# One core, four layers: a six-place weight ring that runs across the layers, boundary transposes inside the last products, every lo split on VectorE

## The reference

```python
for l in range(2):                                   # block A
    z = rms_norm(x, norm_mix[l]) @ w_in[l]           # 1024 -> 4768 columns
    c_q, c_kv, k_pe, hq, hf, hi, hg, g_a, g_b = split(z)
    y_a = mla_mixer(c_q, c_kv, k_pe, ...) @ w_proj_a[l]      # 8 heads of 96, causal
    y_b = hgrn2_mixer(hq, hf, hi, hg, ...) @ w_proj_b[l]     # 4 heads of 128, decay per channel
    x = x + (sigmoid(g_a) * y_a + sigmoid(g_b) * y_b) @ w_out[l]
    h = rms_norm(x, norm_ffn[l])
    x = x + (silu(h @ w_gate[l]) * (h @ w_up[l])) @ w_down[l]   # 1024 -> 2816 -> 1024
for l in range(2):                                   # block B
    q, k, v, z, xbc, dt = split(rmsnorm(x, ...) @ w_in_2[l])    # 1024 -> 3344 columns
    attn = dilated_attention(rotary(q), rotary(k), v)
    y = ssd_chunked(silu(conv4(xbc)), softplus(dt), ...) * silu(z)
    x = x + concat(attn, rmsnorm(y)) @ w_out_2[l]
    x = x + swiglu(rmsnorm(x, ...), w_gate_2[l], w_up_2[l], w_down_2[l])
return rmsnorm(x, final_norm)
```

## Time and profile before

| what | value |
|---|---|
| median of 3 runs | 1556.57 us (1555.61 to 1557.41) |
| profiled execution, span | 1555.7 us |
| PE busy / PEld busy | 1479.3 us (95%) / 1258.1 us (81%) |
| DVE / ACT / POOL busy | 946.3 us (61%) / 787.6 us (51%) / 198.3 us (13%) |
| mean granted TensorE clock | 0.988 |
| moved from HBM | 243.52 MB, 157 GB/s over the span |

### The profile page before, as it was taken

How to read it: one execution, slowest core, us unless ns; L and a number is a source line. 1 busy time by engine, 2 the same in 40 slices (tenths; PEclk the granted TensorE clock), 3 DMA queues, 4 the chain that set the end, 5 groups by cost and what they waited for, 6 DMA issues and landing times.

```text
span 1555.7 us, 23669 instructions
## 1 busy us (share of the span) xinstructions
PE 1479.3 (95%) x7525; PEld 1258.1 (81%) x7525; DVE 946.3 (61%) x1306; ACT 787.6 (51%) x1228; POOL 198.3 (13%) x146
## 2 busy tenths in 40 slices
PE   4998999999989799999999999999999999999997
PEld 4877887888888688788888988888887988888886
DVE  3577775555455887655554497755554487755554
ACT  4574445444366554544445665544444565554443
POOL 1033300000010432000002232000002223000000
PEclk9998999999999999999999999999999999999999
DMA  6653255655555523465655343465655343455553
GB/s 183 197 155 109 82 163 162 192 191 185 171 174 153 159 84 122 150 202 185 191 183 173 103 133 119 136 191 188 189 189 161 112 139 110 149 172 184 185 189 107
DMA packets 180347, 245.92 MB, mean 158 GB/s; under 512 B 21008, under 2 KB 131984, under 8 KB 180240
## 3 DMA queue, kind: packets, MB, share of 16 engines
q1 hardware_dynamic: 180240, 244.61, 50.3%
HBM read 243.52 MB, written 1.05 MB: 157 GB/s over the span
## 4 chain that ended last, share of the span: by engine, by line
PE 82%; DVE 8%; issue 5%; ACT 3%; SPq 1%; DMA 0%; DVEq 0%; ACTq 0%; POOL 0%; POOLq 0%
PE acc L578 15%; PE acc L580 15%; PE acc L579 15%; PE misc L578 9%; PE misc L580 9%; PE misc L579 9%; PE misc L643 2%; DVE w_lo L1289 2%; PE misc L736 2%; DVE arena L1612 2%; PE misc L859 1%; PE misc L653 1%; DVE arena L1370 1%; PE misc L807 1%; ACT w_hi L928 1%
## 5 line engine op out<-in xcount | busy, mean ns | idle before, releaser
L1289 DVE TENSOR_TENSOR w_lo<-w_raw,w_hi 128x1024 fp32r<-128x1024 f32 (+3 forms) x420 | 504.7, 1210 | 333.3 <-ACT w_hi L928 331.0
L928 ACT ACTIVATE w_hi<-w_raw 128x1024 fp32r<-128x1024 f32 (+3 forms) x472 | 481.2, 1029 | 321.0 <-PE misc L580 162.8
L578 PE MATMUL acc<-w_hi,h_hi 128*128 128x512 f32 (+3 forms) x832 | 315.7, 379 | 38.4 <-DVE w_lo L1289 23.9
L580 PE MATMUL acc<-w_hi,h_lo 128*128 128x512 f32 (+3 forms) x832 | 307.6, 370 | 0.0
L579 PE MATMUL acc<-w_lo,h_hi 128*128 128x512 f32 (+3 forms) x832 | 307.3, 369 | 0.0
L578 PE MATMUL misc<-w_hi,h_hi 128*128 128x512 f32 x640 | 253.8, 396 | 0.5
L580 PE MATMUL misc<-w_hi,h_lo 128*128 128x512 f32 x640 | 249.7, 390 | 0.0
L579 PE MATMUL misc<-w_lo,h_hi 128*128 128x512 f32 x640 | 249.2, 389 | 0.0
L578 PEld LDWEIGHTS acc<-w_hi,h_hi 128*128 128x128 f32 x832 | 160.4, 193 | 66.3 <-DVE w_lo L1289 27.5
L1832 POOL TENSOR_TENSOR w_lo<-w_raw,w_hi 128x1024 fp32r<-128x1024 f32 (+2 forms) x52 | 113.3, 2186 | 766.7 <-ACT w_hi L928 766.7
L578 PE MATMUL acc<-w_hi,st_hi 128*128 128x512 f32 (+1 forms) x456 | 177.9, 390 | 0.9 <-DVE w_lo L1289 0.9
(11 more groups left out here) (199 smaller groups left out, 1360.9 us busy)
## 6 DMA issues: line engine op xcount, KB each, us to landing
w_raw<-in_w_in SPq DMA_DIRECT2D x92, 512.0 KB, 4.4
w_raw<-in_w_gate SPq DMA_DIRECT2D x176, 256.0 KB, 2.9
w_raw<-in_w_up SPq DMA_DIRECT2D x176, 256.0 KB, 3.1
w_raw<-in_w_down SPq DMA_DIRECT2D x88, 512.0 KB, 3.3
w_raw<-in_w_out SPq DMA_DIRECT2D x40, 512.0 KB, 3.4
w_raw<-in_w_in SPq DMA_DIRECT2D x32, 388.0 KB, 3.2
w_raw<-in_w_in SPq DMA_DIRECT2D x16, 336.0 KB, 5.0
w_raw<-in_w_proj_a SPq DMA_DIRECT2D x8, 512.0 KB, 3.4
```

The lines of the kernel that those rows point to most:

```text
L578: pe.matmul(dst, hi[:, k, cols], rhs_hi, start=first, stop=False)
L580: return pe.matmul(dst, lo[:, k, cols], rhs_hi, start=False, stop=last)
L928: act.activation(w_hi[:, s % RING, 0:w], w_raw[:, s % RING, 0:w], ACT.Copy)\
L1289: dve.tensor_tensor(w_lo[:, s % RING, 0:w], w_raw[:, s % RING, 0:w], w_hi[:, s % RING, 0:w].bitcast(F32), ALU.subtract)\
```

## The change

The layer loops and the feed-forward loop are written out, so that all four layers are one straight program and slots have one running number g. The ring gets six places and `LOOK` becomes 5; splits for the next layer's slots are made during the last feed-forward steps. GpSimd makes no lo any more. SP loads the next layer's parameters in feed-forward step 4. nT0 and nT1 of the next layer stand ahead of the last three matmuls of the last down product, nT2 and nT3 inside or behind the first slot of the layer; mT2 and mT3 stand behind the first gate/up slot. The last down product does its left half for both slots first. `lbc` is computed once. The scratch for dynamic transfers is set to 2048.

```diff
-RING = 4
+RING = 6
-POOL_LO = ({0, 1, 2, *range(ORD[0].slot_no["gate1", 1], ORD[0].slot_no["gate3", 3] + 1, 2)},
-           {0, 1, 2, *range(ORD[1].slot_no["xd0", 0], ORD[1].slot_no["wo1", 1] + 1, 2)})
-LOOK = 3
+LOOK = RING - 1
+        for i in (2, 3):
+            self.before["misc", f"mT{i}"] = self.ffn0 + 1
...
-        nT0 nT1 nT2 nT3 qkv0 qkv0 qkv1 ...
+        nT0 nT1 qkv0 nT2 nT3 qkv0 qkv1 ...
...
@@ SP: ahead of each load; feed-forward loads
+            def freed(g):
+                if g >= RING:
+                    sp.wait_ge(*DV_.of("lo", g - RING))
...
+                    if i == 4 and layer != LAYERS[-1]:
+                        params(LAYERS[LAYERS.index(layer) + 1])
@@ PE: run_slot, gate_up, last_down
+                    if name == "qkv0" and k == 2:
+                        shared(layer, "nT2")
+                        shared(layer, "nT3")
...
+                        if i == 0 and q == 1:
+                            shared(layer, "mT2")
+                            shared(layer, "mT3")
...
+            def last_down(g):
+                pe.wait_ge(*DV_.at(layer, "fT10"))
+                pe.wait_ge(*DV_.of("lo", g))
+                half_down(g, 10, 0)
+                pe.wait_ge(*DV_.of("lo", g + 1))
+                half_down(g + 1, 10, 0).then_inc(*PE.mark("x_half"))
+                half_down(g, 10, 1).then_inc(*PE.slot("used", g))
+                half_down(g + 1, 10, 1, (0,)).then_inc(*PE.mark("x_tile"))
+                if layer != LAYERS[-1]:
+                    ...
+                    shared(after, "nT0")
+                    shared(after, "nT1")
+                half_down(g + 1, 10, 1, (1,)).then_inc(*PE.slot("used", g + 1))
@@ ACT: norm_operand
-                if name == "mT0":
-                    split_until(layer, ORD[layer[0]].chunk_end("wo1") + LOOK)
-                b = wait_bank(layer, name)
-                if kind == "mT":
-                    act.wait_ge(*name_at(PE, layer, "used", ORD[layer[0]].chunk_end("wo1") - 1))
+                if kind == "nT" and i < 2:
+                    split_until(layer, 3)
+                    act.wait_ge(*PE.at(layer, name))
+                    b = misc[ORD[layer[0]].turn[name] % 4]
+                else:
+                    b = wait_bank(layer, name)
@@ DVE: split_until, end of feed_forward, top of body_a
+                n = min(BASE[layer] + n, TOTAL)
+                for g in range(split[0], n):
+                    dve.wait_ge(*AC.of("hi", g))
...
+                dve.wait_ge(*PE.at(layer, "x_half"))
+                residual(layer, [(0, t, acc[t]) for t in range(NT)], ["x_ffn0", "x_ffn1"])
+                if layer != LAYERS[-1]:
+                    ...
+                    norm_operand(after, "nT0")
+                dve.wait_ge(*PE.at(layer, "x_tile"))
+                residual(layer, [(1, 0, acc[2])], ["x_ffn2"])
+                dve.wait_ge(*PE.of("used", BASE[layer] + o.slots - 1))
+                residual(layer, [(1, 1, acc[3])], ["x_ffn3"])
...
-                dve.tensor_copy(lbc[:, 0, :], lbs[:, bass.ds(l, 1), :].rearrange("p a h -> p (a h)"))\
-                    .then_inc(*DV_.mark())
@@ POOL: body_a, the last of its calls
-                    split_until(layer, o.before["misc", f"oH{t}"] + LOOK)
```

More of the change, by code:

```diff
@@ L76, in mark, with slot, of, at @@
         if name is not None:
-            self.table[self.block, name] = self.k
+            self.table[self.layer, name] = self.k
         return self.sem, 1
[L80 to L123, removed]
+    def slot(self, what, g):
+        self.k += 1
+        self.table[what, g] = self.k
+        return self.sem, 1
+    def of(self, what, g):
+        return self.sem, (self.old[what, g] if self.old else 1)
+    def at(self, layer, name):
+        return self.sem, (self.old[layer, name] if self.old else 1)
+    def now(self, layer):
+        return self.sem, self.k
 class Chunk:
@@ L859, in turn, with half_down @@
                             tr = pe.transpose(misc[0][:, at:at + P], f_act[:, t, kk * P:(kk + 1) * P], ident)
-                    tr.then_inc(*PE.mark(f"fT{step}"))
-                def down(s, step, first=False, last=False, j=None, between=None):
-                    pe.wait_ge(*DV_.at(layer, f"fT{step}", j))
+                    tr.then_inc(*PE.mark(f"fT{i}"))
+                def half_down(g, i, half, tiles=range(NT)):
+                    for t in tiles:
+                        at = half * 512
+                        mm = product(acc[2 * half + t][:, :], stat["st"], (g - base) % 2 + (2 if i == 10 else 0), t,
+                                     w_hi[:, g % RING, at:at + 512], w_lo[:, g % RING, at:at + 512],
+                                     i == 0 and (g - base) % 2 == 0, i == 10 and (g - base) % 2 == 1)
+                    return mm
@@ L896, in feed_forward @@
[L896 to L913 removed]
+                down(g + 8, 0)
@@ new lines, in feed_forward @@
+                turn(1)
+                g += 10
+                for i in range(2, FSTEPS - 1):
+                    gate_up(g, i, behind=f"f{i - 1}")
+                    down(g + 4, i - 1)
+                    turn(i)
+                    g += 6
+                gate_up(g, FSTEPS - 1, behind=f"f{FSTEPS - 2}")
+                down(g + 4, FSTEPS - 2, between=FSTEPS - 1)
+                last_down(g + 6)
+            pe.wait_ge(shifted, 1)
+            for layer in LAYERS:
+                PE.begin(layer)
+                for item in ORD[layer[0]].plan:
+                    if item[0] == "slot":
+                        run_slot(layer, item[1], item[2])
+                    elif item[1] in ("nT2", "nT3") and layer[0] == 1:
+                        continue
+                    elif item[1] not in ("mT2", "mT3") and (item[1] not in ("nT0", "nT1") or layer == LAYERS[0]):
+                        shared(layer, item[1])
+                feed_forward(layer)
@@ L1039, in copy_product @@
+                split[0] = max(split[0], BASE[layer] + o.slots)
             def copy_product(layer, name, dst, func=ACT.Copy, rms=None):
@@ L1421, in feed_forward @@
-                split[0] = 0
-                for half, step in enumerate(("x_half", "used-1")):
-                    dve.wait_ge(*PE.at(layer, step))
-                    residual(layer, [(half, t, acc[2 * half + t]) for t in range(NT)],
-                             [f"x_ffn{2 * half + t}" for t in range(NT)])
+                gated(s + 3, 0)
+                turned(s + 4, 0)
+                gated(s + 8, 1)
+                turned(s + 10, 1)
+                s += 10
+                for i in range(2, FSTEPS):
+                    gated(s + 4, i)
+                    turned(s + 6, i)
+                    s += 6
```

434 lines of the change are left out of this document (167 added, 267 removed).

## The result

| what | kernel before | changed kernel |
|---|---|---|
| median | 1556.09 us (1555.29 to 1557.41) | 1548.38 us (1547.32 to 1550.74) |
| ratio, 95% interval | 1 | 0.9948 (0.9934 to 0.9962) |
| profiled execution, span | 1555.7 us | 1549.0 us |
| PE / DVE / ACT / POOL busy | 95 / 61 / 51 / 13% | 95 / 62 / 51 / 6% |
| mean granted TensorE clock | 0.988 | 0.991 |

The kernel became faster by 7.7 us; 17.2 were forecast. Both kernels issue the same 7525 matmuls. So the two profiles can be laid side by side by counting matmuls: for each stretch I take the time between the same two matmuls in both, which holds waits and slow clock together. Gains are positive.

What follows compares the result with a forecast made beforehand. PE was held by waits for lo on VectorE, waits around x's transposes, and a slowed clock. Layer A 11.3, weighed heads 1.5, layer B 11.6, tops 2.3, seams -9.6, ends -0.5 and +0.6 sum to 17.2 us: 1539 us (1528 to 1550).

Steps and rivals of the forecast that it cites:

- the one of layer B: Convolution to cb: VectorE arrives 5.0 us earlier, removing PE's z0 and most cb waits; 5.8 us per layer, 11.6 for both.
- Rival 2: Chains gain only half, as decay and xsd products staying on GpSimd meet VectorE's steps: 12.2 instead of 24.4, 1552 us; chance 0.13.
- Rival 5: The ring of six never fills because raw slots arrive late; z0 and gate0 waits stay, about 1549 us; chance 0.08.
- Rival 1: Seams are free: VectorE has the extra lo done, x arrives earlier, no clock falls; 1528 us; chance 0.13.
- Rival 3: VectorE becomes the bound: slow steps have another cause than GpSimd and added lo stand; about 1573 us; chance 0.09.
- Rival 4: Turns of the feed-forward loops cost instruction fetches hidden by PE's busy time; 31 us more won, 1508 us; chance 0.02.
- The slow steps in A: K heads to qkT: VectorE waits for GpSimd, 8.5 us; chain becomes 22.0 us; with small waits 11.3 us for both layers.
- The two small waits ahead of the chain: Layer A, ahead of VectorE's chain to qkT: these PE waits for lo go, 1.7 us for both layers.
- The 1.5 us at the weighed heads: Layer A, behind weighed heads: of PE's 2.0 us in two waits, 1.5 us taken as gain.
- The tops and seams: Layer tops +4.4, -3.1 and +1.0 us; four wo-to-gate/up seams -9.6 us, from h_lo waits, moved transposes and clock falls.
- the clock's half chances: At each seam and B top, the wait drops the clock in half the cases, costed at 0.9 us.
- The seam's 2.7 us: From wo to gate/up: PE's gap while h_lo of mT0 follows the residuals and one more lo; 2.7 us per seam.

Runs made afterwards that it cites:

- Experiment 7: Changed kernel with a ring of four places and a look-ahead of three instead of six and five: 1548.85 us, ratio 0.9941 to the kernel before.
- experiment 3: Changed kernel with VectorE making h_lo of mT0 and mT1 before the wo1 residuals at the seam: 1532.52 us, ratio 0.9838 to the kernel before.
- experiment 6: Changed kernel with mT2 and mT3 again ahead of the first gate/up slot: 1543.50 us, ratio 0.9905 to the kernel before.
- experiment 10: Changed kernel with GpSimd's four xsd products in layer B cut to eight columns, so output is wrong: 1548.38 us, ratio 0.9938 to the kernel before.
- experiment 11: Changed kernel with level 1 of layer A's recurrence moved behind the scaling of the heads: 1544.04 us, ratio 0.9907 to the kernel before.
- experiment 1: Changed kernel with lo splits in layer B's VectorE chain made two slots ahead, growing back to five: 1542.41 us, ratio 0.9901 to the kernel before.
- experiment 4: Changed kernel with every second lo split of the two mixer stretches put back on GpSimd: 1561.68 us, ratio 1.0021 to the kernel before.
- experiment 9: Changed kernel with edits of experiments 1 to 3, look-ahead tables retuned, h_lo before look-ahead at B tops, recurrence level 1 behind scaling: 1499.59 us, ratio 0.9631.
- experiment 2: Changed kernel with later lo splits in layer A's chain and a smaller look-ahead in early recurrence levels: 1539.39 us, ratio 0.9880 to the kernel before.

## Why the prediction was right in direction and wrong in size

**The step that failed** is the one of layer B: "VectorE arrives 10.8 - 4.6 - 1.2 = 5.0 us earlier", and from it "5.8 us per layer". VectorE's chain to the first M gained 1.45 us, and PE reached the first y product (y0) only 1.2 and 0.6 us earlier within the layer; behind it the clock took 1.6 back in each, so that PE lost 0.4 us in one layer and 1.0 in the other. Three things were wrong in it.

First, the wrong end of the chain was taken. I counted the waits that PE showed, 3.2 us at z0 and 2.0 at cb, as if each could be removed by itself. But y0 behind them waits for M, and in the trace of before PE waited 0.4 us at most there: it arrived just when the chain was done.

```profile
PE misc L816 <- DVE arena L1722: 0.4, 1, 0.4
```

The two waits were slack of one chain. Remove them, and PE runs up against xsT, cb, cr and y: 0.8 + 0.3, 1.5, 1.5 and 1.6 us. Experiment 7 shows the same from the other side: with less stock the waits in B move ahead, and y0 stays.

Second, the chain's own account. Of the 10.8 us by which the convolution was too slow, 2.8 lay in the call at 899.36 us, ahead of a wait for ScalarE and of the stretch above; the chain got 7.6.

```profile
899.36 1.89 DVE L1607 TENSOR_SCALAR arena<-arena,conv 128x256 f32<-128x256 f32 x2 [1.56 <-ACT arena L1169]
901.28 4.30 DVE L1612 SCALAR_TENSOR_TENSOR arena<-arena,conv 128x256 f32<-128x256 f32 x6
...
908.71 1.29 DVE L1315 SCALAR_TENSOR_TENSOR st_lo<-misc,st_hi 128x512 fp32r<-128x512 f32 x2 [0.58 <-ACT st_hi L950]
```

Against that stand 5.4 us of lo (4.6 forecast; the rest is xsd, which slows two of them), and 0.9 more in front of M for ScalarE's exponentials, which the prediction did not look at: 7.6 - 5.4 - 0.9 = 1.3, where 1.45 were measured.

Third, the clock. Its slow stretch used to lie ahead of y0, where PE had to wait in any case; now it follows y0 in both layers (mean clock 0.69 over the 5.5 us behind y0) and costs.

```profile
938.00:944.00 6.00, 6.00 (x30) 5.28 (x30) 3.55 (x7) 2.86 (x6) 0.00 (x0) 0.72 0.27 87
```

This third part is chance: in the profile of experiment 3, whose code is the same there, the slow stretch lies ahead of y0 in one layer (0.73 from 924 to 927 us) and is absent in the other, and xsT to the fourth y product takes 1.6 us less in both; so it does in experiment 6. Without it layer B would have gained 1.8 us in all, still far from 11.6.

Rival 2 had the right place, GpSimd's remaining products, but too large a part: 2.5 us per layer in B (experiment 10), 2.1 in A (experiment 11), where the prediction had 1.2 and 1.5. Its time, 1552, was nearer to the result than the forecast for another reason. Rival 5 named z0 and gate0 waits that stay; they went. Rival 1 needed free seams; they cost 8.5 us. Rival 3 is refuted in A by the chain's 22.3 us; in B the slow steps went too, but its other half, the added lo, holds there: what VectorE sheds it gets back as lo (experiments 1 and 4). Rival 4: PE's 634 instructions between 277 and 417 us fill 140.00 us as in the earlier trace rows, and the stage's gain of 0.4 us per layer goes with the ring (experiment 7). The Trainium skill (Runtime: NRT & Kernel Launch, section Instruction fetch mechanics) would have a fetch at each turn whose target lies outside the loaded window; no run here shows one that PE's work does not hide.

**What held.** The slow steps in A are VectorE waiting for GpSimd's products: the chain, the wait ahead of qkT (5.2 for 4.4 us) and the gain (12.0 for 11.3 us) came out; experiment 4 puts 9.3 us of it back. The two small waits ahead of the chain gave 2.8 us for 1.7 (1.6 by the prediction's own terms). The 1.5 us at the weighed heads did not come: the waits are 2.8 us where the earlier trace rows has 2.0. VectorE makes more lo in the levels there, which I take for the cause; with a look-ahead of three in them 0.5 us are left (experiment 9). The Trainium skill (SBUF — State Buffer, section Who interferes with whom) says that a VectorE instruction with two SBUF inputs and a GpSimd instruction that reads SBUF block each other. The traces agree for VectorE's side, where accumulating steps beside xsd take 6.97 us instead of 2.71; for GpSimd's they show that xsd takes 4.77 us beside these and 6.19 beside two lo, but none has it alone. GpSimd's powers are an exception that the traces show (last section).

The tops and seams came out term by term (the clock's half chances were luck, as two of four seams and one of two B tops had the fall). The waits rest on one method: to write down what stands ahead of h_lo in VectorE's order, and by when its last input exists. The seam's 2.7 us, forecast as the price of the change, was a mere matter of order, as experiment 3 shows; the same look at B's chain, lo by lo, would have given its 5.4 us.

## What to carry to other kernels

A wait that a trace shows is a gain only if the next wait behind it has slack: follow the producer's chain to the product that first had to wait for nothing else, and cost that. Where helpers prepare data ahead of a consumer, a deep look-ahead inside a latency chain is paid in full by the chain; let it shrink to what the consumer needs before the chain ends, and grow again behind it (experiments 1 and 2: 7 and 11 us by the ratios, with no instruction removed). And count time between the same two instructions in both profiles: it showed gains of 2.5 us that the totals hid.

## What the runs showed of the hardware

The granted clock does not fall alike behind the same wait. The four seams have the same wait of 2.7 us in the profiles of the changed kernel and of experiment 1, and the same code; in the first the clock fell behind both A seams and neither B seam, in the second the other way round. Windows around the two A seams, first the changed kernel, then experiment 1 (the clock is the third figure from the right):

```profile
236.00:246.00 10.00, 7.36 (x29) 6.03 (x30) 5.89 (x12) 3.36 (x6) 0.00 (x0) 0.83 0.33 106
639.00:649.00 10.00, 7.54 (x30) 6.18 (x31) 5.87 (x12) 3.38 (x7) 0.00 (x0) 0.83 0.36 107
```

```profile
237.00:247.00 10.00, 7.52 (x37) 6.36 (x38) 5.95 (x12) 4.95 (x10) 0.25 (x2) 1.00 0.34 106
639.00:649.00 10.00, 7.44 (x37) 6.31 (x38) 6.03 (x12) 5.00 (x10) 0.20 (x2) 1.00 0.38 107
```

Each fall costs 1.6 us by stretch. So a wait of this length is worth itself and, in some executions, 1.6 us more. By my estimate from these figures, one profile of a kernel with eight such waits (four seams, two at qkT, two at the tops of B) is uncertain by several us.

GpSimd's powers of 16 columns stand beside VectorE's steps without slowing them: in the changed kernel they run from 105.36 to 108.28 and from 108.60 to 111.68 us, while a lo at 106.56 takes 1.21 us, L1434 0.75 and L1314 1.46. Its products over 512 columns do slow them: two lo beside decay products take 3.69 us, and 2.36 without (experiment 11).
